# Hybrid decoder trunk on one core: side products of the attention on other steps, and products that nobody reads at the head of a layer

## The reference

```python
for l in range(DEPTH):                       # 2
    h = rms_norm(x, mix_norm_g[l])
    u = h @ w_in[l]
    c_q, c_kv, k_rope, z, xs, bs, cs, dt_raw, xr, gate = split_cols(u, IN_SPLITS)
    y_mla = mla_group(...)     # 8 heads, causal attention; q and k products of width 96 per head, v of 64
    y_ssm = mamba2_group(...)  # chunked scan over 8 chunks of 128 tokens
    y_lru = rglru_group(...)
    x = x + concat(rms_norm(y_mla), y_ssm, rms_norm(y_lru)) @ w_out[l]
    ...                        # cross-attention into a memory, then the MLP
```

## Time and profile before

| | |
|---|---|
| median of 3 executions | 3129.14 us (3127.34 to 3129.6) |
| the profiled execution | 3120.94 us, span from first to last instruction 3119.2 us |
| TensorE busy | 2944.1 us, 94% of the span |
| VectorE, ScalarE, GpSimd busy | 50%, 26%, 49% |
| mean granted TensorE clock | 0.978 of full |

### The profile page before, as it was taken

How to read it: one execution, slowest core, us unless ns; L and a number is a source line. 1 busy time by engine, 2 the same in 40 slices (tenths; PEclk the granted TensorE clock), 3 DMA queues, 4 the chain that set the end, 5 groups by cost and what they waited for, 6 DMA issues and landing times. The chain is left out here.

```text
span 3119.2 us, 38234 instructions
## 1 busy us (share of the span) xinstructions
PE 2944.1 (94%) x13824; PEld 2310.9 (74%) x13824; DVE 1555.5 (50%) x1955; ACT 804.1 (26%) x1383; POOL 1528.9 (49%) x1134
## 2 busy tenths in 40 slices
PE   5998999999989999999899998999999899999996
PEld 4875558886778888888778655688858788888885
DVE  7574445204465555544575744551135554455555
ACT  3145552224131111111123454412232211111111
POOL 3332213350367777777543221234404877777773
PEclk9999999999999999999999999999999999999997
DMA  3100001130101111111111000112201111111111
GB/s 145 41 27 5 1 15 60 58 108 18 41 27 54 54 54 50 49 49 47 48 58 38 9 5 1 41 47 85 84 7 47 41 49 48 47 47 50 54 54 68
DMA packets 59990, 143.05 MB, mean 46 GB/s; under 512 B 9072, under 2 KB 11120, under 8 KB 59248
## 3 DMA queue, kind: packets, MB, share of 16 engines
q1 hardware_dynamic: 59888, 141.68, 13.6%
HBM read 135.89 MB, written 5.77 MB: 45 GB/s over the span
## 5 line engine op out<-in xcount | busy, mean ns | idle before, releaser
L1178 PE MATMUL ps<-hm_h,ring 128*128 128x512 f32 x2048 | 642.2, 392 | 14.0 <-issue 9.1
L732 PE MATMUL ps<-hA,wsp 128*128 128x512 f32 x2112 | 496.8, 397 | 39.8 <-POOL wsp L543 36.4
L1861 DVE TENSOR_TENSOR x<-ps,x 128x512 f32<-128x512 f32 x512 | 353.5, 691 | 299.0 <-PE ps L1178 299.0
L732 PEld LDWEIGHTS ps<-hA,wsp 128*128 128x128 f32 x2112 | 403.4, 192 | 128.6 <-POOL wsp L543 37.1
L654 POOL TENSOR_TENSOR ring<-raw,ones 128x512 fp32r<-128x512 f32 x338 | 353.4, 1046 | 277.5 <-PE ps L1178 222.5
L1178 PEld LDWEIGHTS ps<-hm_h,ring 128*128 128x128 f32 x2048 | 386.2, 189 | 107.3 <-issue 27.3
L657 POOL TENSOR_TENSOR ring<-raw,ring 128x512 fp32r<-128x512 f32 x338 | 438.8, 1298 | 26.5
L540 POOL TENSOR_TENSOR wsp<-raw,ones 128x1024 fp32r<-128x1024 f32 x68 | 136.0, 2000 | 627.3 <-PE ps L732 563.4
L1178 PE MATMUL ps<-hm_l,ring 128*128 128x512 f32 x1024 | 400.2, 391 | 0.0
L1162 PE MATMUL ps<-hT,ring 128*128 128x512 f32 x1440 | 331.3, 389 | 0.0
L1162 PEld LDWEIGHTS ps<-hT,ring 128*128 128x128 f32 x1440 | 270.3, 188 | 56.1
(11 more groups left out here) (282 smaller groups left out, 3764.3 us busy)
## 6 DMA issues: line engine op xcount, KB each, us to landing
raw<-in_weight_tiles SPq DMA_DIRECT2D x248, 256.0 KB, 2.6
raw<-in_weight_tiles SPq DMA_DIRECT2D x112, 512.0 KB, 3.2
x<-in_xT SPq DMA_DIRECT2D x1, 4096.0 KB, 15.2
outT<-x SPq DMA_DIRECT2D x8, 512.0 KB, 3.1
wh<-in_head_weights SPq DMA_DIRECT2D x8, 256.0 KB, 2.7
mem_s<-memory_normed SPq DMA_DIRECT2D x2, 1024.0 KB, 4.9
memp<-in_memT SPq DMA_DIRECT2D x1, 1024.0 KB, 4.9
memory_normed<-memp SPq DMA_DIRECT2D x1, 1024.0 KB, 4.2
```

The costliest lines, as they stand in the source:

```text
L732: last = pe.matmul(ps[:, 2 * buf + half, 0:n], w[:, k, col:col + P], rhs(part, k, half * n, n), start=(at_k == 0 and w is w_hi and part == 0),
L1178: last = pe.matmul(ps[:, bank, :], w[:, part, k, (m % 2) * P:(m % 2 + 1) * P], h[k][:, cols_of(half)], start=(k == 0 and part == 0 and h i ...
L1861: dve.tensor_tensor(xm, ps[:, bank, :], xm, ALU.add).then_inc(x_add, 1)
```

## The change

Three edits. The table of side products is reordered: in each pair the second Q goes from step 2 to 1, RB from 1 to 2 and from 9 to 10, the two K from 12 and 14 to 7 and 9, where they share the step with a Q. `keep_y` follows RB by a step. The last load of head weights waits for the side product that is now last to read the buffer. And PE gets products of the identity with a constant triangle, whose result nobody reads: 26 at the head of each layer, before the first pair of tiles, and 14 behind that pair.

```diff
--- before.py
+++ after.py
@@ -101,10 +101,10 @@
     out = []
     for c in range(PAIRS):
         a = 2 * c
-        plan = [(0, "Q", 2 * (a + 2)), (1, "RB", a - 1), (2, "Q", 2 * (a + 2) + 1), (3, "EL", a), (4, "EA", a),
-                (5, "CB", a), (6, "TR", a), (7, "Q", 2 * (a + 3)), (8, "Y", a), (9, "RB", a),
-                (10, "Q", 2 * (a + 3) + 1), (10, "EL", a + 1), (11, "EA", a + 1), (12, "K", a + 2),
-                (12, "CB", a + 1), (13, "TR", a + 1), (14, "K", a + 3), (15, "Y", a + 1)]
+        plan = [(0, "Q", 2 * (a + 2)), (1, "Q", 2 * (a + 2) + 1), (2, "RB", a - 1), (3, "EL", a), (4, "EA", a),
+                (5, "CB", a), (6, "TR", a), (7, "Q", 2 * (a + 3)), (7, "K", a + 2), (8, "Y", a), (9, "K", a + 3),
+                (9, "Q", 2 * (a + 3) + 1), (10, "RB", a), (10, "EL", a + 1), (11, "EA", a + 1), (12, "CB", a + 1),
+                (13, "TR", a + 1), (15, "Y", a + 1)]
         for step, kind, i in plan:
             if (kind in ("Q", "K") and c == PAIRS - 1) or (kind == "RB" and i < 0):
                 continue
@@ -487,7 +487,7 @@
                         elif c == 2:
                             sp.wait_ge(ip_ps, 6)
                         else:
-                            sp.wait_ge(side_ps, SIDE_NO["K", 3] + 1)
+                            sp.wait_ge(side_ps, SIDE_NO["Q", 7] + 1)
                         load_heads(c)
                     sp.wait_ge(o_ps, 2 * PAIRS * 2)
                     load_pair(R_OUT, 2 * R_OUT)
@@ -745,6 +745,11 @@
                     def of(h):
                         return lambda part, k, c, n: h[:, part, k, c:c + n]
 
+                    def idle_products(n, bank=5):
+
+                        for _ in range(n):
+                            pe.matmul(ps[:, bank, 0:P], ident[:, :], tri_le[:, :], start=True, stop=True)
+
                     def sum_cols(i, src, bank=7):
 
                         pe.wait_ge(sum_ready, i + 1)
@@ -800,7 +805,9 @@
                         pe.wait_ge(t_free[s], u + 1)
                         tile3(s, s, of(hA)).then_inc(t_ready[s], 1)
 
+                    idle_products(26)
                     pair(0, U_IN, of(hA), hooks=chunk_ready)
+                    idle_products(14)
                     sum_cols(N_MIX, ss)
                     halves(T_CKV, 2, lambda: spread(N_MIX, bank=6))
                     whole(T_MISC)
@@ -1721,7 +1728,7 @@
                         for kind, i in side_at(n):
                             if kind in BY_DVE:
                                 side_dve(kind, i)
-                        if n > 1 and n % NBLK == 1:
+                        if n > 2 and n % NBLK == 2:
                             keep_y(n // NBLK - 1)
                     recip_sums(2 * PAIRS - 1)
```

## The result

The changed kernel takes 3135.74 us (median of 9 executions) against 3129.14 us of the kernel before on the same chip (9 executions): 1.0027 times as long, 95% interval 1.0018 to 1.0036. It is slower, by 6.6 us between the medians and by 5.6 to 11.3 us by the interval; 3141, 12 us more than before, was forecast, with a range of 3128 to 3149.

What follows compares the result with a forecast made beforehand. TensorE, busy 94% of the span, was taken as the bound, so changes count where it waits or runs at the lower clock. 6.9 + 3 - 1.5 + 3.9 = 12.3 us on 3129.1 gave 3141 us, range 3128 to 3149.

Steps and rivals of the forecast that it cites:

- The two K: Attention, K at steps 7 and 9: new waits +3.05, old waits gone -0.7 and -1.2 a pair; six pairs, +6.9 us.
- step 7: Attention: K behind Q waits 1.26 us, since VectorE's two rotations of Q set its start.
- step 9: Attention: Q waits 1.7 us, since K's copies stand on ScalarE behind the exponential of unit 10.
- RB a step later: Attention: moving RB lengthens waits in every pair, with EL's 0.75 new in the last; 1.5 us a layer, +3.
- The clock at a pair's end: Second layer's attention: one of two half-clock pair ends goes, -1.5 us; bounds 0 and -3.1.
- The head: Start of each layer, unread products: `sum_cols` later by 1.6 and 2.3 us, together +3.9; bounds +2.0 and +8.
- stall at the fifth chunk: Second layer's head: at full clock TensorE catches up with `hA` and loses 1.9 us of the 3.1 gained.
- the cold case: Head: clock not raised, pair ends as now, 14 products lie open; +2.4 us second layer, +3.0 first.
- The collision that I forecast: Head: GpSimd's split meets VectorE's last addition, 2.80 us instead of 1.23; `sum_cols` 1.6 us later.
- C: Rival: faster, 3115 us; the 1.85 wait goes whole, its successors are hidden, clock -3.1, head +3.9; chance 0.08.
- D: Rival: unread products hold full clock through the head and beyond, -3.1 and -2 us by layer; 3122 us, chance 0.08.
- B: Rival: waits move but cost little, head +2.0, both half-clock ends go (-3.1); 3129 to 3135 us, chance 0.2.

Runs made afterwards that it cites:

- experiment 2: The kernel before plus the 26 + 14 unread products at the head of each layer, side-product table as before: 3127.50 us, ratio 1.0001.
- Experiment 5: New side-product table without unread products, with ScalarE copying K ahead of the exponential at step 9, against the kernel before: 3129.87 us, ratio 1.0010.
- experiment 6: The kernel before with only RB and the second Q moved, both K left at steps 12 and 14, no unread products: 3131.7 us, ratio 1.0016.
- experiment 1: The kernel before with the attention edit alone (new side-product table, keep_y a step later), no unread products: 3135.08 us, ratio 1.0036.
- experiment 7: The kernel before with 26 unread products ahead of the first pair, none behind it: 3128.41 us, ratio 1.0008.
- experiment 9: The kernel before with 44 unread products ahead of the first pair and 14 behind it, side products as before: 3129.61 us, ratio 1.0014.

## Why the prediction was right, and where it was off

The direction was right and the time is in the range, but the size was not: the sum was +12.3 us, where the interval of the runs is +5.6 to +11.3. The attention's mechanism was right; at the head a step failed, and the products came to nothing measurable (experiment 2) where +3.9 was forecast.

**The two K** (+6.9). Right by mechanism and nearly in size. Forecast and measured waits: step 7 1.26 and 1.14; step 9 1.7 and 1.70; RB 0.35 and 0.19; EL 0.75 and 0.56, with today's 0.88 gone; up to the scores behind step 10 pair 1 lost 3.15 beyond K's own work and RB's shift, for 3.05. Behind step 12 it won 0.68 (0.7 forecast), and at its end 1.34 (1.2). These are differences of starts in the two timelines of pair 1; together the two K cost 3.15 - 0.68 - 1.34 = 1.13 there, for 1.15. Experiment 5 shows the cause at step 9.

**RB a step later** (+3). Mis-sized: 3.8 to 4.3 by experiment 6. In pair 1 it cost 0.5 where I had 0.3; the new wait is that of the outputs at step 4 [0.50, row 311.01], which I had counted among the waits that go in exchange. The last pair lost 0.96 for 0.75. In all the attention lost 1.6 (pair 0 of experiment 1 against before, both with the same clock) + 1.63 + 1.75 + 0.96 = 5.9 a layer at equal clock, for 4.95. That is 11.9 in both; the two K with six times the 1.13 of pair 1 and RB with 3.8 to 4.3 give 10.6 to 11.1 of it, and the rest is not assigned.

**The clock at a pair's end** (-1.5). I let one of the two half-clock ends go; both went, and none came back in any of the profiles without K at step 14. A pair with such an end took 61.29 us for 59.73, 1.56 more. So the term was -3.1, at its bound. What I left out is that the clock also falls at other places of the attention: in the first layer its first stretch at half clock was 6.8 us long for 3.4 before, in the second 3.4 for none, +2.5 together in these two profiles. The other kernels with K at step 14 had one to six such ends in their profiles (four of them had four).

**The head** (+3.9). Here a step failed, the clock at the pair's start. "They are hidden unless the clock stays at half" led me to a pair at full clock, a stall at the fifth chunk and a last addition of 2.8 us in the second layer. I had written that the clock may fall again before the pair, but for the first layer only. It fell in both: the idle time of 3.32 us (4.47 in the first layer) stood between. So the cold case came (the pair at half clock as before, the 14 products open behind it): +2.9 and +2.1, for +2.3 and +1.6. The collision that I forecast is real, but came in other kernels: in the second head of experiment 7, and in experiment 1, first layer, where the pair ended early by itself (POOL, DVE and PE rows of the timeline):

```profile
59.84 2.00 POOL L540 TENSOR_TENSOR wsp<-raw,ones 128x1024 fp32r<-128x1024 f32 x1 [4.61 <-PE ps L732]
60.12 2.80 DVE L1528 TENSOR_TENSOR ss<-ss,rs 128x1024 f32<-128x1024 f32 x1
...
63.03 3.58 PE L752 MATMUL ps<-ones,ss 128*128 128x1 f32 x16 [3.35 <-DVEq L1530]
```

The split meets the last addition, 2.80 for 1.23, and TensorE idles 3.35 us; a pair that ends early then has its `sum_cols` 27.3 us behind its start, no earlier than the cold one with 14 products. Two figures of this step were off besides. The stall at the fifth chunk, 1.9 forecast, was 0.20 in the second head of experiment 7 and nothing in that of 9, where the pair started 1.3 and 3.0 us later than before. And GpSimd's split L540 takes 1.89 us at least in the profile of before, not the 1.75 that I wrote.

**What I did not see.** Two terms, of opposite sign. The start of the second layer's pair came 2.5 us later. And the stage behind the head was 1.8 and 3.5 us shorter: its mean clock was 0.99 and 0.97 and is 1.00 now, in both layers. Over all profiles this stage takes 173.9 us in the mean with the 14 products behind the pair (10 heads) and 175.8 with no products there (14 heads; the 26 ahead alone, with 179, are left out). One part of that the traces show: in the six heads where TensorE idled 3.3 us or more ahead of `sum_cols`, the clock stood at half for 6.8 to 10.3 us from within 0.8 us of `sum_cols` on, and the stage took 177.3 to 179.3 us; in the ten heads with the 14 products TensorE idled there 0.46 us at most, and no stretch at half clock follows within 50 us. But before had idle times of 0.25 and 0.77 only, and experiment 2, with the same products as the changed kernel, gave nothing back (176.1 and 174.4). So what shortened this stage in the changed kernel's profile is not shown to be the products.

The parts of the profile are thus: attention +11.9 - 3.1 + 2.5 = +11.3 for +8.4, products +7.5 - 5.3 = +2.2 for +3.9, everything else +0.5, together 14.0. That the forecast of 12.3 lies near it is luck in part: one term too small, others of opposite sign that I did not have, and a fast profile of before to compare with. By the ratios the products are worth nothing (1.0001, with the interval of 0.1% to either side), the attention edit +11 us (7 to 16) and the whole +8 (6 to 11).

**Rivals.** C needed ScalarE to copy K first; even so (experiment 5) the kernel is not faster. D failed at the head, where the clock fell again (0.50 at the pair's start); a gain stands behind the head in the one profile, not in that of experiment 2. B had both half-clock ends right, but not the waits: they cost 5.9 us a layer. Its +2.0 for the head is near the +2.2 that is left of 7.5 and -5.3, by other terms. The range took in the whole of B (3129 to 3135), not its greater part.

**Open.** Why a longer instruction stream goes with a later start. The first split waits for a weight tile, whose load is issued 0.6 to 1.1 us later than in before and takes up to 1.8 us longer; that instruction loads compete with it is argued, not shown: their number in that gap is the same, only the second comes earlier. Why the clock falls at one to six of the pair ends with the same wait of 1.85 is open as well. The kernel with the 26 products alone has stages of 179 us behind its heads, where TensorE idled 3.35 and 3.58 us ahead of `sum_cols`; why it is not slower in the median for that is open.

## What to carry to other kernels

A wait for a copy does not vanish when its product is moved: it goes where the product stands next, and grows when another product shares that step, since the two then wait for one bank in turn; look for a step where outputs or another long product cover the copy, and count what stands before the copy on its own engine. Here the K at steps 8 and 12 gained 0.3%, part of it by the clock, where both beside a Q, with RB a step later, lost 0.4%. Products that only keep the clock up must leave little idle time before the work that they are for; even then they did not pay here (experiment 9, 1.0014 with 1.0002 to 1.0025), since they cost at their place and the pair behind them started later. And one profile of each kernel is not enough for a difference of this size: the same code gave spans 5 us apart.

## What the runs showed of the hardware

- Products whose result nobody reads raised the granted clock from half to full (0.50 in 1564.64:1567.64, 1.00 in 1568.00:1574.50). This is the row that the prediction missed for the rule of the Trainium skill ("TensorE: Matmul & The Clock Gate", Part 1) that activity releases the clock; the trace agrees. After 3.32 us idle the next stretch had 0.50 again. Of the eight pairs behind such products, five began behind idle times of 2.46 to 4.47 us and were at half clock at their start or at most 0.9 us behind it, and three began behind 0.00 to 1.66 us and ran at full clock to their end.
- Every kernel with at least 14 more products per layer had 66 instruction loads for 65, wherever they stood, and began the second layer's first pair 1.3 to 3.0 us later than the kernel before. The extra load is not in the gap before that pair.
- A GpSimd split beside VectorE's addition of two operands makes the latter 2.80 us for 1.23, with and without unread products. The Trainium skill ("SBUF — State Buffer", section on the two sides) has the two take the port in turn; the rows agree: in experiment 1 the addition starts 0.28 us behind the split and ends 1.08 behind its end, so it waited for what was left of the split.
